# Two-layer decoder step: the last gate's tanh and product, the memory maxima and two quarters of gate products at other places in four engines' orders

## What is computed

```
z = rms_norm(x, norm) @ w_in                 # [mixer | its gate | memory query | memory gate]
ym = softmax(rms_norm(qm) . mem_k) . mem_v * silu(gm)      # 4 heads, 256 memory tokens
layer A: y = (windowed mean of u over 2,4,8,16 tokens - u) @ mix_w * scale * silu(g)
layer B: y = sliding-window attention (window 128, 12 query and 4 key heads, sinks) * silu(g)
x = x + concat(y, ym) @ w_out
```

## Time and profile before

| | |
|---|---|
| median of three runs | 1689.85 us |
| the profiled execution's own time | 1692.14 us |
| its span, first to last instruction | 1690.4 us |
| PE busy | 1546.4 us, 91% |
| PEld | 1184.8 us, 70% |
| DVE | 834.1 us, 49% |
| ACT | 544.2 us, 32% |
| POOL | 505.7 us, 30% |
| mean granted TensorE clock | 0.967 of full speed |
| DMA | 75 GB/s over the span |

### The profile page before, as it was taken

How to read it: one execution, slowest core, us unless ns; L and a number is a source line. 1 busy time by engine, 2 the same in 40 slices (tenths; PEclk the granted TensorE clock), 3 DMA queues, 4 the chain that set the end, 5 groups by cost and what they waited for, 6 DMA issues and landing times.

```text
span 1690.4 us, 32455 instructions
## 1 busy us (share of the span) xinstructions
PE 1546.4 (91%) x12867; PEld 1184.8 (70%) x12867; DVE 834.1 (49%) x1777; ACT 544.2 (32%) x1352; POOL 505.7 (30%) x369
## 2 busy tenths in 40 slices
PE   5848999999999999978999999999999999999976
PEld 3627888887888888864766757667476675767744
DVE  3856554555455455433634636346263462735522
ACT  2353241322324233221524315143151431614330
POOL 0116333444434335231323223232232322214110
PEclk9879999999999999998999999999999999999986
DMA  9043121221312213295010010100101001010040
GB/s 389 32 150 119 56 102 63 88 100 66 135 51 100 76 76 129 80 382 235 2 51 1 1 51 1 51 1 1 51 1 51 1 1 51 1 51 1 5 181 26
DMA packets 25121, 127.38 MB, mean 75 GB/s; under 512 B 2455, under 2 KB 3095, under 8 KB 12518
## 3 DMA queue, kind: packets, MB, share of 16 engines
q1 hardware_dynamic: 24830, 124.88, 19.1%
q10 hardware_dynamic: 144, 0.37, 0.1%
HBM read 87.64 MB, written 39.74 MB: 75 GB/s over the span
## 4 chain that ended last, share of the span: by engine, by line
PE 40%; issue 23%; DVE 16%; POOL 13%; ACT 6%; DMA 1%; POOLq 0%; DVEq 0%; SPq 0%; ACTq 0%
PE ps_z L655 16%; PE ps_z L689 14%; PE ps_z L666 3%; ACT ph_sb L1462 3%; DVE ph_sb L2082 2%; POOL w_x_sb L2295 2%; DVE tiny_sb L2085 2%; DVE ph_sb L2109 2%; POOL ph_sb L2360 2%; POOL tiny_sb L2264 1%; POOL ph_sb L2358 1%; POOL big_sb L2269 1%; DVE xn_sb L1608 1%; DVE tiny_sb L1672 1%; PE ps_p L1034 1%
## 5 line engine op out<-in xcount | busy, mean ns | idle before, releaser
L666 PE MATMUL ps_z<-xn_sb,w_in_sb 128*128 128x256 f16 (+1 forms) x4752 | 502.4, 264 | 12.9 <-DVE gate_sb L1687 6.7
L666 PEld LDWEIGHTS ps_z<-xn_sb,w_in_sb 128*128 128x128 f16 x4752 | 426.0, 98 | 76.6 <-issue 15.1
L689 PE MATMUL ps_z<-pm_sb,w_out_sb 128*128 128x256 f16 x3072 | 349.5, 274 | 16.5 <-DVE gate_sb L1687 16.5
L689 PEld LDWEIGHTS ps_z<-pm_sb,w_out_sb 128*128 128x128 f16 x3072 | 299.6, 99 | 57.4 <-DVE gate_sb L1687 18.7
L2264 POOL TENSOR_TENSOR tiny_sb<-tiny_sb 128x8 f32<-128x8 f32 (+5 forms) x74 | 108.6, 1468 | 609.6 <-DVE tiny_sb L1654 302.8
L655 PE MATMUL ps_z<-w_in_sb,xn_sb 128*128 128x512 f16 (+2 forms) x840 | 181.7, 376 | 0.0
L1198 ACT ACTIVATE scr_sb<-ps_z,tiny_sb 128x256 f32<-128x256 f32 (+2 forms) x94 | 42.6, 490 | 377.6 <-PE ps_z L655 296.8
L655 PEld LDWEIGHTS ps_z<-w_in_sb,xn_sb 128*128 128x128 f16 (+1 forms) x840 | 82.9, 99 | 94.1 <-issue 0.2
L1645 DVE TENSOR_REDUCE tiny_sb<-scr_sb 128x8 f32<-128x512 f32 (+3 forms) x64 | 38.0, 593 | 221.1 <-ACT scr_sb L1198 139.3
L1728 DVE SCALAR_TENSOR_TENSOR x_buf_sb<-ps_z,tiny_sb,x_buf_sb 128x512 f32<-128x512 f32 x64 | 48.0, 750 | 120.0 <-PE ps_z L689 120.0
L655 PE MATMUL ps_z<-w_x_sb,xn_sb 128*128 128x512 f16 (+1 forms) x408 | 93.7, 391 | 10.8 <-issue 5.8
(11 more groups left out here) (287 smaller groups left out, 2109.5 us busy)
## 6 DMA issues: line engine op xcount, KB each, us to landing
x_buf_sb<-x SPq DMA_DIRECT2D x18, 1024.0 KB, 5.0
w_x_sb<-w_b SPq DMA_DIRECT2D x18, 1024.0 KB, 6.3
x<-x_buf_sb SPq DMA_DIRECT2D x9, 1024.0 KB, 4.1
y<-x_buf_sb SPq DMA_DIRECT2D x9, 1024.0 KB, 3.9
parts<-ph_sb SPq DMA_DIRECT2D x16, 512.0 KB, 3.0
parts<-w_x_sb SPq DMA_DIRECT2D x16, 512.0 KB, 3.6
w_in_sb<-parts SPq DMA_DIRECT2D x8, 1024.0 KB, 10.9
w_out_sb<-w_mem SPq DMA_DIRECT2D x4, 1024.0 KB, 18.6
```

Of the source, the lines that this page charges most:

```text
L666: last = mm(ps_z[:, b, half * NT:half * NT + n], w_split[:, g, ws, kc, half * P:(half + 1) * P], xs[:, x, kc, 0:n], start=(kc == 0 and ws ...
L689: done = mm(ps_z[:, b, half * NT:(half + 1) * NT], w_out_split[:, g, ws, kc, half * P:(half + 1) * P], gated_parts[:, x, kc, :], start=sta ...
```

## The change

No instruction is added or taken away; five groups of them stand elsewhere.

- TensorE, B: half of g0's first half (input chunks 0 to 3) stands ahead of the transposes `q_transposes_b(1, 0)`; a quarter of g2's second half (chunks 0 and 1) stands ahead of `window_values(2)`.
- ScalarE, A: the order `high_b(1,1)`, `mem_exps(0)`, `mem_exps(1)`, `tanh(g0)` becomes `mem_exps(0)`, `tanh(g0)`, `mem_exps(1)`, `high_b(1,1)`.
- ScalarE, B: `tanh(g2)` ahead of `window_exps(5)`.
- VectorE, A: `low_b(1,1)` goes from ahead of the memory maxima to behind `mem_inverse(1)`, and `silu(g0)` ahead of `mem_inverse(1)`.
- VectorE, B: `silu(g2)` goes from behind `window_back(5)` to ahead of `window_weights(4)`.

```diff
@@ -1067,8 +1067,9 @@
                     T.wait_read(pe, "B", t, "qT01")
                     mem_scores("B", t, 0, qT_b, 6)
                     window_scores(t, p, 0)
+                    split_features("B", t, "g0", 4, halves=(0,), kcs=range(0, 4))
                     q_transposes_b("B", t, 1, 0)
-                    split_features("B", t, "g0", 4, halves=(0,))
+                    split_features("B", t, "g0", 4, halves=(0,), kcs=range(4, 8))
                     T.wait_read(pe, "B", t, "qT10")
                     q_transposes_b("B", t, 1, 1)
                     window_scores(t, p, 1)
@@ -1092,10 +1093,11 @@
                     window_transposes(t, 2)
                     mem_values("B", t)
                     window_scores(t, p, 4)
+                    split_features("B", t, "g2", 6, halves=(1,), kcs=range(0, 2))
                     window_values(t, p, 2)
                     window_transposes(t, 3)
                     window_scores(t, p, 5)
-                    split_features("B", t, "g2", 6, halves=(1,))
+                    split_features("B", t, "g2", 6, halves=(1,), kcs=range(2, 8))
                     window_values(t, p, 3)
                     for g in range(4):
                         pe.wait_ge(wout_in[g], 32)
@@ -1386,10 +1388,10 @@
                     pooled_inputs(2)
                     from_t("A", t, "qT", qT_a[:, :, :], ps_t[:, :].rearrange("p (c n) -> p c n", c=2))
                     high_b(t, 1, 0)
+                    mem_exps("A", t, 0)
+                    tanh("A", t, "g0", halfunit_a[:, 4:5])
+                    mem_exps("A", t, 1)
                     high_b(t, 1, 1)
-                    mem_exps("A", t, 0)
-                    mem_exps("A", t, 1)
-                    tanh("A", t, "g0", halfunit_a[:, 4:5])
                     tanh("A", t, "g1", halfunit_a[:, 5:6])
                     mem_weights("A", t, 0, 0)
                     mem_weights("A", t, 0, 1)
@@ -1508,9 +1510,9 @@
                     gate_high("B", t, 1, 3)
                     window_exps(t, 4)
                     window_prev(t, 5)
+                    tanh("B", t, "g2", halfunit_b[:, 6:7])
                     window_exps(t, 5)
                     gate_high("B", t, 2, 1)
-                    tanh("B", t, "g2", halfunit_b[:, 6:7])
                     squares_x("B", t, 0, p, (it + 6 + p) * 16)
                     gate_high("B", t, 3, 2)
                     x_high("B", t)
@@ -1925,13 +1927,12 @@
                     low_b(t, 0, 0)
                     low_b(t, 0, 1)
                     low_b(t, 1, 0)
-                    low_b(t, 1, 1)
                     for blk in range(NBLK):
                         mem_max("A", t, blk)
-                    for blk in range(NBLK):
-                        mem_inverse("A", t, blk)
-
+                    mem_inverse("A", t, 0)
                     silu("A", t, "g0", 1, 0)
+                    mem_inverse("A", t, 1)
+                    low_b(t, 1, 1)
                     silu("A", t, "g1", 2, 2)
                     window_differences(t)
                     mix_gated(t, 0)
@@ -2161,10 +2162,10 @@
                     window_back(t, 4)
                     window_front(t, 5)
                     window_gated(t, 3)
+                    silu("B", t, "g2", 9, 4)
                     window_weights(t, 4)
                     gate_low("B", t, 1, 3)
                     window_back(t, 5)
-                    silu("B", t, "g2", 9, 4)
                     gate_low("B", t, 2, 1)
                     window_gated(t, 4)
                     window_weights(t, 5)
```

## The result

| | kernel before | changed kernel |
|---|---|---|
| median of the runs | 1690.76 us (1685.21 to 1700.75, 6 runs) | 1670.01 us (1666.26 to 1673.57, 6 runs) |
| ratio | | 0.985, 95% interval 0.9821 to 0.9879 |
| profiled execution / span | 1692.14 / 1690.4 us | 1671.8 / 1670.0 us |
| undisturbed tile of the A loop / B loop | 71.7 / 102.7 us | 70.5 / 101.2 us |
| A tile / B tile, mean of seven | 72.69 / 104.66 us | 71.44 / 102.3 us |

What follows compares the result with a forecast made beforehand. TensorE's matmuls were busy for 91% of the span, so only its standing still or running slower could be won. B 11.0, A 9.2 and clock 2.4 us sum to 22.6 off 1689.85: 1667 us, range 1660 to 1679.

Steps and rivals of the forecast that it cites:

- B, tanh and product: B loop: moving g2's tanh and product earlier removes out1's 2.06 us wait; norm(5) comes next; 1.38 us a tile gained.
- The hold at norm(5): B loop: gate_low of pair 1 holds GpSimd's norm(5) through the shared port, costing 0.4 us a tile.
- The rival without holds: VectorE and GpSimd don't hold each other at the new places: 1.80 us a B tile, 1662 us in all; chance 0.15.
- Quarters: B loop: g0's products ahead of q_transposes_b(1,0) given nothing, bounds 0 and 0.86 us; g2's fill window_values(2)'s 0.65 us wait.
- A: A loop: both TensorE waits go, GpSimd's window sums end 0.84 us earlier; 1.15 us a tile, 9.2 us in all.
- DMA behind low_b(1,1): A loop: the last parts write goes out 6.6 us later, with the next two weight loads behind it; costs nothing.
- The tiles of a loop are alike to 0.1 us: Both loops: one tile's timeline was taken to stand for all eight.
- Clock: B loop: TensorE's clock halves after the 2.06 us wait in three tiles, 4.7 us; half expected back, 2.4 us.
- Sum: Whole kernel: 11.0 (B) + 9.2 (A) + 2.4 (clock) = 22.6 us off, giving 1667 us.

Runs made afterwards that it cites:

- E5: The changed kernel with gate_low of pair 1 moved behind window_gated(4) on VectorE in the B loop; 1665.48 us, ratio 0.9826.
- E4: The kernel before with only the two pieces of gate products in B moved, tanh and product of g2 left in place; 1696.84 us, ratio 0.999.
- E3: The kernel before with only g2's tanh and product in B moved, all gate products left in place; 1680.28 us, ratio 0.9881.
- E1: The kernel before with only the A loop's new orders on ScalarE and VectorE; 1683.37 us, ratio 0.9917.
- E6: The changed kernel with A's tanh(g0) back behind mem_exps(1) and silu(g0) back behind mem_inverse(1); 1665.61 us, ratio 0.981.
- E7: The changed kernel with A's low_b(1,1) moved from behind mem_inverse(1) to behind the last gate_low; 1665.02 us, ratio 0.9815.
- E2: The kernel before with all B edits only: the quarters of gate products and g2's tanh and product; 1680.18 us, ratio 0.9887.
- E11: The changed kernel measured once more, on the same chip as E9 and E10; 1667.39 us, ratio 0.9823 to the kernel before.
- E9: E8 with window_back(5) moved ahead of gate_low of pair 3 on VectorE in B; 1662.69 us, ratio 0.9802 to the kernel before.
- E8: The changed kernel with the edits of E5 and E6 together; 1665.52 us, ratio 0.9816 to the kernel before.
- E10: E9 with GpSimd's first gains in A waiting for VectorE's last low part of the output weights; 1660.60 us, ratio 0.9785 to the kernel before.

## Why the prediction was right, point by point

- **B, tanh and product.** Right in its chain and its size. Forecast 1.38 us a tile, measured 1.4 (102.7 to 101.2 or 101.3). transposes(5) waits 1.04 us (forecast 1.0), transposes(4) 0.23 (0.3), norm(5) lasts 1.43 (about 1.5). On the clock of the earlier trace rows transposes(5) starts at 1162.62, forecast 1162.70.
- **The hold at norm(5)**, for which the rows of before had no gate_low beside GpSimd: E5 takes it away, and 0.4 us a tile with it. The rival without holds had the price right, 1.80 us: E5's tile is 1.8 shorter than before's.
- **Quarters.** Worth nothing: E4 and E3. Of the bounds 0 and 0.86 us the lower was right, and the wait did go to ScalarE's read of qT10.
- **A.** Forecast 1.15 us a tile, measured 1.2 in the changed kernel and in E1. The scaling took 1.14 us (forecast 1.1), low_b 2.19 (2.2) from 453.98, which is 455.23 on the clock of the earlier trace rows (455.24), the window sums came 0.86 us earlier (0.84). The early tanh and product of g0 cost 0.2 us (E6); the forecast counted no gain from them, but no cost either.
- **DMA behind low_b(1,1).** No cost, as forecast; E7 delays it by 16 us more for none.
- **"The tiles of a loop are alike to 0.1 us"** is not so. They alternate (71.7 and 74.0 us in A, 102.7 and 104.9 in B), and the B tiles with a stretch are longer again. What is alike in all of them are the waits, which is what the sum needed; the tiles where the pass changes became shorter too, by 1.1 to 1.5 us in A.
- **Clock, the term that was mis-sized.** Forecast 2.4 us, half of 4.7 for three stretches. (Of their windows the one from 1055 us reads 0.74, not 0.66; its stretch starts at 1057.4.) In the profiles of the three kernels with the wait of 2.06 to 2.4 us at out1 (before, E1, E4) there are 12 stretches at 1.2 GHz at it, in 24 B tiles, and two elsewhere; in those of the three with B's gate moved (E2, E3, changed) there is none there in 24 tiles, and one elsewhere. E5 to E11 have none there either, in 56 more tiles. Each costs some 1.6 us of its tile (102.7 becomes 104.3). So all of it went, not half, 4.7 us; and the fourth stretch of before, at the change of pass, which the forecast didn't count, is missing from the changed kernel's profile too, though nothing of the change stands there. Together 4 x 1.6 = 6.4 us in this pair of profiles, of which one is chance as far as is known: E2, with the same B loop, has a stretch at that place. The B tile's mean fell by 2.4 us (to 102.3, forecast 103.2) and not by 1.4.
- **Sum.** The loops gave more than forecast: A 8 x 1.2 and B 8 x 1.4 and 6.4 of clock, 27.2 us against 22.6. But the profiles differ by 20.4 us, and the medians by 20.8 us. The missing 6.8 us is in two places whose code is unchanged: 3.8 us ahead of the first A store (2.6 more instead of 1.2 less; 3.2 of them explained below), and 3.6 in the sample layer between the loops (from the last A store to the first B store 2.2 us more, where the first B tile should have made it 1.4 less); the other tiles gave 0.6 us more than the rounded numbers. Between those two stores the clock is at 1.2 GHz for 13.7 us before and for 23.9 in the changed kernel. Over the thirteen profiles it is so for 7 to 24 us, and among the ten with B's gate moved the length goes with it: 155.7 to 157.1 us in the three with 6.8 us of it (E2, E5, E7), 162.3 and 162.5 in the two with 23.9 (E6, changed). That fits the missing 3.6 us; no experiment tests it, and why a run gets more or less is open. The forecast came out within 3 us because two errors of the opposite sign met, one of them a piece that the change doesn't touch. That part is luck.

## What to carry to other kernels

A wait that is filled with other work is worth only what the next chain allows. Ask who is second (here norm(5)), write down when it ends, and take the difference: that gave both tiles to 0.1 us, where the sum of the waits removed (2.7 us in B) would have been twice too much. In an order written by hand, look for a VectorE instruction with two SBUF operands beside the GpSimd instruction that the next matmul waits for, and price the hold: moving it away gave 0.4 us a tile (E5), but starting that GpSimd instruction 0.6 us earlier, held again, gave 0.2 more (E9). And measure a tile by the distance of its stores: 0.2 us a tile shows there, while medians of runs here spread over 3 us or more.

## What the runs showed of the hardware that was not expected

**3.2 us in unchanged code, by who starts first.** At the start of the A loop, VectorE forms the last two low parts of the output weights while GpSimd begins its gains as soon as a DMA has landed. The timeline over all engines, first before:

```profile
125.24 2.35 DVE L1763 SCALAR_TENSOR_TENSOR w_out_sb<-gate_sb,tiny_sb,w_out_sb 128x2048 f16<-128x2048 f32 x1
...
125.92 5.14 POOL L2295 TENSOR_TENSOR w_x_sb<-w_x_sb,small_sb 128x2048 f32<-128x2048 f32 x1 [4.22 <-DMA w_x_sb<-w_b]
...
138.41 4.84 PE L666 MATMUL ps_z<-xn_sb,w_in_sb 128*128 128x256 f16 x24 [4.93 <-DVE pm_sb L1648]
```

then the changed kernel:

```profile
125.07 9.21 POOL L2296 TENSOR_TENSOR w_x_sb<-w_x_sb,small_sb 128x2048 f32<-128x2048 f32 x2 [3.33 <-DMA w_x_sb<-w_b]
...
125.29 5.53 DVE L1765 SCALAR_TENSOR_TENSOR w_out_sb<-gate_sb,tiny_sb,w_out_sb 128x2048 f16<-128x2048 f32 x1
...
141.64 3.60 PE L666 MATMUL ps_z<-xn_sb,w_in_sb 128*128 128x256 f16 x16 [9.33 <-DVE pm_sb L1650]
```

If VectorE begins first (125.24 against 125.92), its first instruction takes 2.35 us; if GpSimd does, by 0.22 us, it takes 5.53, all behind it is 3.2 us late, and TensorE, idle for 4.9 us in tile 0 before, is idle for 9.3. In the five profiles where VectorE was first (before, E1, E4, E5, E7) TensorE goes on at 138.3 to 138.9 us, in the seven where GpSimd was (changed, E2, E3, E6, E8, E9, E11) at 141.6 to 142.3. The order is close: VectorE was ahead by 0.09 us in E5 and behind by 0.01 us in E2. The changed kernel, the only one with two profiles, was late in both, so it isn't shown that one and the same kernel gets now one order, now the other. E10 makes GpSimd wait:

```profile
130.69 7.16 POOL L2296 TENSOR_TENSOR w_x_sb<-w_x_sb,small_sb 128x2048 f32<-128x2048 f32 x2 [8.54 <-DVE w_out_sb L1765]
...
137.86 4.45 PE L666 MATMUL ps_z<-xn_sb,w_in_sb 128*128 128x256 f16 x24 [4.36 <-DVE pm_sb L1650]
```

The Trainium skill, page "SBUF — State Buffer", section "Who interferes with whom", describes such an exclusive lock between these two engines. The rows agree: 2.35 us becomes 5.53 where GpSimd was first. What releases GpSimd's instruction in both kernels is a landing DMA, so a difference of tenths of a microsecond in it can decide the order. In E10 both of VectorE's instructions take 2.35 us, and TensorE goes on at 137.9.

**An instruction on four columns is held too.** The scaling of 128x4 took 1.14 us beside GpSimd's instruction and 0.17 alone, in each of the seven A tiles. It ended at 448.55, GpSimd's 3.29 us at 448.53: what counted was how much of GpSimd's instruction was left, not the own size.

**Half the clock behind a wait of 2 us.** At out1's wait of 2.06 to 2.4 us TensorE went to 1.2 GHz for 3.4 us in 12 of 24 tiles; behind the 1.04 us that took its place, or the 0.4 to 0.7 us of E3, E5 and E8 to E10, in none of 80. With 1.6 us of clock a wait of 2.06 us cost nearly twice its length in those tiles, and a gain worked out from the wait alone is too small. But the length of the wait isn't all: at the changes of pass TensorE stands for 1.6 to 2.3 us in every kernel, 78 times in the thirteen profiles, and a stretch followed only 9 times. What makes the difference was not found.
